# Last steps of the expert stage and the norm that opens the next layer

## The reference, cut to what matters

```python
def hier_moe(h, w_grp, w_exp, w1, w3, w2):      # 32 experts, 2 per token
    ...
    for e in range(N_EXPERTS):
        a = jax.nn.silu(ht @ w1[e]) * (ht @ w3[e])
        y = y + combine[:, e:e + 1] * (a @ w2[e]).astype(jnp.float32)
    ...
x = x + gt2[:, None, :] * hier_moe(h2, ...)     # first block's last line
...
def rmsnorm_2(x, g):
    y = xf * lax.rsqrt(jnp.mean(xf * xf, axis=-1, keepdims=True) + NORM_EPS)
    return (y * g).astype(x.dtype)
h = rmsnorm_2(x, norm_gains[0]);  z = h @ w_in  # splits: lru_x, lru_gate, q, k, v, swa_gate
```

## Time and profile before

| | us |
|---|---|
| median of 3 runs | 2454.22 (2449.99 to 2456.52) |
| profiled execution, its own time | 2448.66 |
| its span | 2446.8 |
| TensorE matmuls busy | 2104.9 (86%) |
| VectorE busy | 1214.5 (50%) |
| ScalarE busy | 898.2 (37%) |
| HBM read | 691.66 MB, 284 GB/s over the span |

### The profile page before, as it was taken

One profiled execution on the slowest core, in us unless ns is written; L12 is line 12 of the kernel. 1 busy time (PEld: TensorE's weight loads), 2 busy tenths in 40 slices (PEclk: granted clock), 3 DMA queues, 4 the chain that ended last, 5 costly groups with the idle time before them and its releaser, 6 DMA issues.

```text
span 2446.8 us, 38264 instructions
## 1 busy us (share of the span) xinstructions
PE 2104.9 (86%) x14524; PEld 1399.7 (57%) x14524; DVE 1214.5 (50%) x2205; ACT 898.2 (37%) x1382; POOL 0.2 (0%) x4
## 2 busy tenths in 40 slices
PE   5699998986887888887878887899989799998987
PEld 1377776862222222222222222799889799997887
DVE  1544785454333333333333334647875554477555
ACT  1333434441112111221112221546865444466543
POOL 0000000000000000000000000000000000000000
PEclk9899999998999999999999999899999899998999
DMA  9988775966999999999999997364445455543442
GB/s 378 404 310 300 255 279 194 340 245 273 422 422 421 422 422 422 422 422 422 422 422 422 422 422 299 113 199 146 137 140 179 129 172 182 181 139 107 134 128 97
DMA packets 135046, 695.44 MB, mean 284 GB/s; under 512 B 14992, under 2 KB 15120, under 8 KB 85264
## 3 DMA queue, kind: packets, MB, share of 16 engines
q1 hardware_dynamic: 134928, 693.81, 74.2%
HBM read 691.66 MB, written 2.10 MB: 284 GB/s over the span
## 4 chain that ended last, share of the span: by engine, by line
PE 50%; DMA 37%; DVE 7%; ACT 4%; issue 2%; SPq 1%; DVEq 0%; ACTq 0%
PE acc L1000 34%; DMA ring<-in_w 33%; DMA land<-in_stream_a 4%; PE acc L997 3%; PE psS L1226 3%; PE psO L1050 3%; DVE WL L1662 1%; ACT WH L1378 1%; SPq L880 1%; PE psM L1081 1%; ACT SB L1448 1%; DVE HL L1672 0%; PE psT L946 0%; PE psM L1214 0%; PE psM L1050 0%
## 5 line engine op out<-in xcount | busy, mean ns | idle before, releaser
L1000 PE MATMUL acc<-HH,WH 128*128 128x256 f32 x2552 | 749.0, 293 | 40.7 <-DVE HL L1684 15.4
L1000 PE MATMUL acc<-HH,WL 128*128 128x256 f32 x2552 | 727.9, 285 | 0.0
L1000 PE MATMUL acc<-HL,WH 128*128 128x256 f32 x2552 | 727.4, 285 | 0.0
L1662 DVE TENSOR_TENSOR WL<-land,WH 128x1024 fp32r<-128x1024 f32 (+1 forms) x350 | 425.6, 1216 | 420.6 <-ACT WH L1378 416.5
L1000 PEld LDWEIGHTS acc<-HH,WH 128*128 128x128 f32 x2552 | 495.3, 194 | 81.7 <-issue 14.5
L1000 PEld LDWEIGHTS acc<-HH,WL 128*128 128x128 f32 x2552 | 495.9, 194 | 3.3 <-issue 2.2
L1000 PEld LDWEIGHTS acc<-HL,WH 128*128 128x128 f32 x2552 | 495.4, 194 | 0.0
L1378 ACT ACTIVATE WH<-land 128x1024 fp32r<-128x1024 f32 (+1 forms) x350 | 368.0, 1051 | 248.6 <-PE acc L1000 198.9
L1226 PE MATMUL psS<-ring,low 128*32 128x512 f32 x2048 | 282.3, 664 | 148.9 <-DMA ring<-in_w 126.7
L1226 PEld LDWEIGHTS psS<-ring,low 128*32 128x32 f32 x2048 | 53.4, 113 | 339.3 <-DMA ring<-in_w 253.0
L2046 DVE TENSOR_REDUCE SB<-psT 128x128 f32<-128x512 f32 x32 | 22.1, 692 | 389.0 <-PE psT L1236 389.0
(11 more groups left out here) (326 smaller groups left out, 1989.0 us busy)
## 6 DMA issues: line engine op xcount, KB each, us to landing
ring<-in_w SPq DMA_DIRECT2D x384, 1024.0 KB, 24.1
land<-in_stream_a SPq DMA_DIRECT2D x284, 512.0 KB, 7.5
land<-in_stream_bc SPq DMA_DIRECT2D x246, 512.0 KB, 3.8
land<-in_stream_bc SPq DMA_DIRECT2D x12, 384.0 KB, 3.2
X<-in_xT SPq DMA_DIRECT2D x1, 2048.0 KB, 15.8
out<-low SPq DMA_DIRECT2D x4, 512.0 KB, 2.7
cst<-in_const SPq DMA_DIRECT2D x1, 1538.0 KB, 12.3
low<-in_w_pool SPq DMA_DIRECT2D x1, 1024.0 KB, 4.9
```

Source lines behind the costliest of these rows:

```text
L1000: mm = pe.matmul(bank[:, 0:S], w[:, kk, :], h[:, rows[kk], :], start=(z == 0 and i == 0), stop=stop)
L1662: ins = dve.tensor_tensor(WL[:, q % PARTS, 0:n], land[k][:, p % LAND[k], 0:n], WH[:, q % PARTS, 0:n].bitcast(F32), ALU.subtract)
```

## The change

What it does: (1) bankO is multiplied by a tile GB (the gate gt2 laid out in rows, made once by a VectorE copy, four matmuls and a ScalarE copy near the end of list A) when VectorE evacuates it to OE, and the scatter outputs are added into X itself; YT is gone. (2) The scatter of tile i-1 stands between the up-products: slot s, then output s. Outputs are numbered so that output m holds chunks `chunks_of(m)`. (3) VectorE takes the OE evacuation from ScalarE, and makes the first selection ahead of the clears. (4) The last tile's scatter belongs to BC: an addition "res", two HH copies and one 128x512 square for each output; X is not scaled by the norm's factor. The squares are added on VectorE (7 additions of 128x512), summed by two matmuls ("ssm") placed, with the two that turn the factor into a column ("rcol"), between the halves of the product bk1. (5) The factor is applied to bk, bs, lx, lg by a VectorE evacuation that multiplies by RT, to bv by ScalarE's scale, and to the queries in the softmax scale. bq stays a plain copy. (6) In BC the ring `land` moves to ring slots 0 to 3, WH and WL to slots 3 to 7, HH and HL to slots 7 to 11; the stream of layer two starts when the last tile's slots 0 to 3 are used, ScalarE's high parts after its slots 0 to 7. The first four low parts are computed by GpSimd. The count w_used starts at 12 (SLOTS), given by the clear of bankO, so each wait on it is written 12 higher.

```diff
+def evac_by(x):
+    return "dve" if x[0] in ("bk", "bs", "lx", "lg") else "act"
+def chunks_of(m):
+    return (8 * (m // 4) + m % 4, 8 * (m // 4) + m % 4 + 4)
 def order_bc():
-    o.load(1)
+    o.load(4, by="pool")
+    o.add("dve", "zero_b")
+    o.add("dve", "weigh_out")
+    for m in range(8):
+        o.add("pe", "scat", m)
+        for c in chunks_of(m):
+            o.add("act", "hh", "moe", c)
+        o.add("act", "sqm", m)
+    split = [c for m in range(8) for c in chunks_of(m)]
+    for m in range(8):
+        o.add("dve", "res", ("moe", m))
+        if m > 1:
+            o.add("dve", "hl", "moe", split.pop(0))
+    for c in split:
+        o.add("dve", "hl", "moe", c)
+    for m in range(1, 8):
+        o.add("dve", "sqsum", ("moe", m))
     o.misc.append(("ssum", "moe"))
-    for n in range(KD):
-        o.add("dve", "res", ("moe", n))
-        o.add("act", "sq", ("moe", n))
-        o.add("pe", "ss", ("moe", n))
-    o.load(1)
-    o.norm_input("moe")
-    o.load(2)
+    o.add("dve", "ssum", "moe")
+    o.add("act", "sqrtn", "moe")
+    o.add("dve", "rstd", "moe")
+    o.misc.append(("rcol",))
+    o.add("dve", "rcol")
     for n in range(2):
-        o.proj(("bk", n))
+        o.proj(("bk", n), after="sums" if n else None)
 # SyncE
-                    sp.wait_ge(moe["w_used"], i * SLOTS + (s + 1 - SLOTS))
+                    sp.wait_ge(moe["w_used"], i * SLOTS + (s + 1))
-            sp.wait_ge(moe["w_used"], tiles * SLOTS)
+            sp.wait_ge(moe["w_used"], tiles * SLOTS + 4)
             stream(1, BC, t["stream_bc"], tiles)
 # TensorE, the loop
                     mm.then_inc(moe["w_used"], 1)
+                    if s == 0:
+                        pe.wait_ge(moe["oe_ready"], i + 1)
+                        pe.wait_ge(moe["scj_ready"], i + 1)
+                    pe.wait_ge(moe["y_added"], i * 8 + s + 1)
+                    scatter(s).then_inc(moe["y_full"], 1)
...
-                scatter(i)
+                spread(i)
+                pe.wait_ge(moe["y_added"], i * 8 + 10)
+                gather_t(i + 1)
                 pe.wait_ge(moe["at_ready"], i + 2)
...
-                pe.wait_ge(moe["y_added"], i * 8 + 10)
-                gather_t(i + 1)
-                spread(i)
-            scatter(tiles)
             run(1, BC)
 # ScalarE
-                act.wait_ge(moe["w_used"], i * 12 + 12)
-                act.wait_ge(moe["y_full"], i * 8 + 8)
-                act.activation(OE, bankO, ACT.Copy).then_inc(moe["oe_ready"], 1)
-            act.wait_ge(moe["y_added"], tiles * 8 + 10)
+            act.wait_ge(moe["w_used"], tiles * SLOTS + 8)
             run(1, BC)
 # VectorE
-            dve.memset(OE, 0.0) ...; dve.memset(YT[:, 0:8, :], 0.0) ...; dve.memset(YT[:, 8:16, :], 0.0) ...
             pick(0, True)
+            dve.memset(bankO, 0.0) ...; (SJ in two halves, AT, H1T, H3T, SL1 as before)
             weigh(0, True)
             with dve.Fori(0, tiles) as i:
+                dve.wait_ge(moe["w_used"], i * SLOTS + SLOTS)
+                dve.tensor_tensor(OE, bankO, GB, ALU.mult).then_inc(moe["oe_ready"], 1)
                 pick(i + 1)
+                for m in range(8):
+                    add_out(m, i)
...
+                    elif what == "evac":
+                        bank = acc[o.acc.index(("proj", x)) % 2]
+                            ins = dve.tensor_tensor(W(at)[:, 0, :], bank[:, 0:S], RT, ALU.mult)
 # GpSimd
+                pool.tensor_tensor(WLs[1][:, q % PARTS, 0:n], land[1][:, p % LAND[1], 0:n],
+                                   WHs[1][:, q % PARTS, 0:n].bitcast(F32), ALU.subtract)
```

More of the change, by code:

```diff
@@ L204, in mix_head, with proj @@
         self.misc.append(("ssum", name))
-    def proj(self, x, halves=None, post=None, loads=1, between=None, first=0):
+    def proj(self, x, halves=None, post=None, loads=1, between=None, first=0, after=None):
         if halves is None:
@@ L220, in proj @@
                     between()
+                if after:
+                    self.add("pe", "ssm")
+                    self.add("pe", "rcol")
         self.acc.append(("proj", x))
-        self.add("act", "evac", x)
+        self.add(evac_by(x), "evac", x)
         if x[0] == "wi":
@@ L464, in order_a @@
         o.add("act", "h2", c)
+    o.add("dve", "gt2rows")
     o.add("pe", "router")
@@ L737, in program @@
         unit_in = [[sem(f"unit_in{k}_{i}") for i in range(LAND[k])] for k in range(2)]
-        done = [{e: sem(f"{e}_done{k}") for e in ("pe", "act", "dve")} for k in range(2)]
+        done = [{e: sem(f"{e}_done{k}") for e in ("pe", "act", "dve", "pool")} for k in range(2)]
         act_link, dve_link = sem("act_link"), sem("dve_link")
@@ L768, in program @@
         lam2 = small[:, 50:56]
+        rcol, rq = small[:, 202:204], small[:, 204:206]
         jst = small[:, 112:144].rearrange("p (b k h) -> p b k h", b=2, k=4)
@@ L981, in product @@
                     last = i == 1
-                needs(k, "dve", o, "lo", q)
+                needs(k, o.lo_by[q], o, "lo", q)
+                WH, WL, HH, HL = WHs[k], WLs[k], HHs[k], HLs[k]
                 wh, wl = (z[:, q % PARTS, cols].rearrange("p (k m) -> p k m", k=len(rows)) for z in (WH, WL))
-                terms = [(a, b, c, kk) for kk in range(len(rows)) for a, b, c in ((wh, HH, 0), (wl, HH, 1), (wh, HL, 2))]
+                order = range(len(rows))
+                if name == "bk":
+                    order = [c - rows[0] for m in range(4 * i, 4 * i + 4) for c in chunks_of(m)]
+                terms = [(a, b, c, kk) for kk in order for a, b, c in ((wh, HH, 0), (wl, HH, 1), (wh, HL, 2))]
                 normed = {("k", 0): "x", ("bk", 0): "moe", ("cq", 0): "wb"}.get(x)
@@ L2061, in _ @@
             dve.wait_ge(moe["y_added"], tiles * 8 + 2)
-            for m in range(8):
-                add_out(m, tiles)
-            dve.wait_ge(moe["y_added"], tiles * 8 + 10)
             dve.wait_ge(moe["j_ready"], tiles + 2)
             run(1, BC)
+        @block.gpsimd
+        def _(pool):
+            for count, (what, q) in enumerate(BC.steps["pool"]):
+                assert what == "lo"
+                if count:
+                    pool.wait_ge(done[1]["pool"], count)
+                p = BC.halves[q]
+                n = BC.pieces[p][2]
+                pool.wait_ge(done[1]["act"], BC.at["act"][("hi", q)])
+                pool.tensor_tensor(WLs[1][:, q % PARTS, 0:n], land[1][:, p % LAND[1], 0:n],
+                                   WHs[1][:, q % PARTS, 0:n].bitcast(F32), ALU.subtract).then_inc(done[1]["pool"], 1)
 def _unit(w):
```

236 lines of the change are left out of this document (150 added, 86 removed).

## The result

The changed kernel takes **2434.4 us** (median of 4 runs, 2431.95 to 2441.22), the kernel before 2454.97 beside it: ratio 0.9929, 95% interval 0.9913 to 0.9945. Taken again in another series it had 2437.5 and 0.9935 (0.9921 to 0.9949). The forecast was 2417: the direction was right, the gain about half of what was forecast, and the time lies just outside the range.

The account below looks back on a forecast made before the run. It took the expert loop as DMA-bound between two serial chains, and later layers as TensorE-bound. Terms -6.2 - 31.0 + 3.5 = -33.7 gave 2415 from the profile or 2420.5 from the median; forecast 2417, range 2404 to 2434.

Parts of the forecast that it names:

- What bounds the kernel, and the period of a tile: Expert loop: DMA-bound at 422 GB/s, 29.83 us a tile, with serial chains around it; layers behind bound by TensorE.
- rival 3: Expert loop: TensorE's chain at the lower clock outlasts the DMA, +55 us, 2470; chance 0.04.
- Part 1: Loop entry: selection ahead of the clears lets slot 0 be used earlier, -6.2 us (bounds -7.5 and -4).
- Part 2: Inside the expert loop: reordered matmuls stay hidden under the DMA, cost 0.
- steady chain of 23.3: Expert loop: TensorE's estimated time per tile in the new order at full clock, 6.5 us below 29.83.
- Part 3: Loop exit to bk1's second half: shorter chain gains 32.6 us, -31.0 after the clock (bounds -25 and -36).
- The 1.6 for the clock: Second half of bk1: 1.6 us taken from the exit's gain because it runs partly at the lower level.
- Part 4: Exit: GpSimd computes the first four low parts in time for TensorE, cost 0.
- rival 1: Exit: GpSimd and VectorE block each other, making VectorE about 3.3 us late, 2420; chance 0.18.
- Part 5: Stage of bs, lx, lg: 24 evacuations moved from ScalarE to VectorE cost +3.5 us (bounds 0 and +10).
- rival 2: Stage of bs, lx, lg: VectorE becomes the bound, evacuations and late banks show, +10 to +14, 2426; chance 0.13.
- three signs of being wrong: Tile period over 30 us, pause before bk1's second half over 10 us, bs/lx/lg stage growing by over 8 us.

Follow-up runs that it names:

- e3: Changed kernel with scatter products and additions back at their old place inside the loop; 2441.4 us, ratio 0.9954 to the kernel before.
- e0: Changed kernel timed again without any edit; 2437.5 us, ratio 0.9935 to the kernel before.
- e1: Changed kernel with bs, lx, lg evacuated raw by ScalarE and multiplied by the factor in SBUF by VectorE; 2427.4 us, ratio 0.9898 to the kernel before.
- e2: e1 without the 24 factor multiplications, so bs, lx, lg stay unscaled; 2425.9 us, ratio 0.9891 to the kernel before.
- e5: Changed kernel with GpSimd writing zeros instead of computing the first four low parts; 2438.4 us, ratio 0.9933 to the kernel before.
- e6: Changed kernel with squares summed by TensorE, column products behind bk1 and the root's table loaded early; 2433.4 us, ratio 0.9918 to the kernel before.
- e4: Changed kernel with five idle TensorE products ahead of the first gather; 2434.6 us, ratio 0.9921 to the kernel before.
- v4: v3b plus one idle 128x256 product in each pause ahead of slot 0; 2419.7 us, ratio 0.9868 to the kernel before.
- v2: Changed kernel with the edits of e1, e4 and e6, and two of four low parts moved back to VectorE; 2420.3 us, ratio 0.9862 to the kernel before.
- e8: Changed kernel with eight idle TensorE products ahead of the first gather; 2434.8 us, ratio 0.9917 to the kernel before.
- v3b: v2 with eight idle products instead of five, a repeat timing; 2419.2 us, ratio 0.9865 to the kernel before.

## Why the prediction was wrong, step by step

**What bounds the kernel, and the period of a tile**: right. 29.82 us at 422 GB/s; rival 3 is out.

**Part 1, -6.2**: measured -6.9. Right, though about 1.0 of it is not the change's: the router's five small products behind the mark ran at the full level in after (0.39 us each) and at the lower one in before (0.61). In e3, which has the same entry as after, they took 0.61 again, and slot 0 came 28.5 behind the mark.

**Part 2, "Cost 0"**: wrong by 6 us (5.4 over the other profiles). I compared the steady chain of 23.3 with 29.83. The first tiles are not steady: the queue is empty, and what counts is how soon the first slots are given back. With a scatter between slots at the lower level the first two came 3.9 us apart, against the 2.49 that the DMA needs for one, and all eight were used within 18.0 us, against 7.1 in before; the down-products began 23.7 us behind slot 0 instead of 17.9. The rate was 352 and 383 GB/s from 580 to 590 where before had 424 and 423. From slot 2 on the slots came every 2.06 us, faster than the DMA needs them, and the rate was low even so; what holds it down with few slots in the queue is not shown. Order and clock can be set side by side, slot 0 to landed: old order, full level 929.5 (before); old order, lower level 931.0 (e3); new order, lower level 934.6 to 935.5 (after, e0, e1, e2, e5, e6); new order, full level 930.8 and 932.5 (e4, v4). So the order costs some 4 at the lower level and 1 to 3 at the full one. The chain I had added up was short as well: a slot and its scatter take 2.06 at the full level, not 1.83. The new order is still worth having: it saves 6.7 at the exit (e3).

**Part 3, -32.6 before the clock**: measured -28.3. Of the 4.3 missing, 1.9 is a term that I had put at nothing: I set L = 1501.5 where the DMA rate falls and let TensorE use the last slot at once, but by the spacing of the slots TensorE can use it only at 1503.5. In before a scatter hid these 2 us, so counted from the landing as TensorE sees it the exit before was 60.0 long, not 62.0; in the new exit they stand on the chain. The other 2.4 are behind that, 31.8 instead of 29.4 (the terms I gave add up to 29.1): 1.8 is VectorE, late with HL and the sums (26.6 instead of 24.8), most of which e5 takes back. The 1.6 for the clock was about right (4.81 against 3.0).

**Part 4, "0"**: four low parts in 9.79 us, 2.45 each, were in time for TensorE. Their effect on VectorE was rival 1, given 3.3 us and measured at 1.4 to 1.8. The Trainium skill, "SBUF — State Buffer", section "Who interferes with whom", says that a VectorE instruction with two SBUF inputs and a GpSimd instruction that reads SBUF contend, and that one which only writes doesn't. The trace agrees: two HL took 1.74 us beside GpSimd's subtraction, and HL took 0.48 beside its writing of zeros and alone. The estimate of 2.3 us, worked out from the Trainium skill, "GPSIMD Engine Reference", section 3.1, stands beside 2.45 measured.

**Part 5, "+3.5 (bounds 0 and +10, all 24 exposed)"**: this is the step that failed. Measured 13.9 (e2), beyond its bound. I had written that "a bank is now free only when VectorE, in order, comes to it", and then priced it by the instructions' own time, 0.43 each, with the halves in WH/WL as a cushion. Those cushion TensorE against late weights, not against a late bank: with two banks, TensorE stops after one product. The price is what stands ahead of the exit in VectorE's queue: in e0 9.4 us of waits at three places, 7.8 in the first profile. To that come matmuls at the lower level, some 1.7 us more for each 48 behind the two long waits and 1.5 behind the second wait on HL. It is rival 2's size (+10 to +14). Rival 2 named two causes together, VectorE's load and the late banks; e1, which changes the second and leaves the first, took 10.2 back, e2 the other 3.7. Its headline, VectorE as the bound, was the smaller part; its "each late bank shows" was the larger. A reading in this part was off too: from 1720 to 1780 TensorE lost 2.0 us in before, not 3. Of the three signs of being wrong that I had named, only the last came: the period is 29.82, the pause before bk1's second half is 6.7 us, and the stage of bs, lx and lg grew by 11.7.

The sum: -6.2 forecast became -6.9 (0.7 better), 0 became +6.0, -32.6 became -28.3, +5.1 became +16.4: 21.0 us worse behind the router. The medians move by 15.4 to 20.6 and the profiles behind the router by 12.7. Only one profile of before exists, and its 2448.66 lies 6.3 below the median beside it; where in before the remaining 3 to 8 us lie stays open.

## What to carry to other kernels

Before an exit from PSUM is moved to another engine, list what stands ahead of it in that engine's order: the bank waits for all of it, and with two banks the matmul engine stops. A factor can be applied one step later, in SBUF, at almost the same cost in instructions, and no bank waits for it. And a stage bound by DMA still has a start: price the first tile with an empty queue and at the level that the profile shows there, not by the steady period.

## What was unexpected of the hardware

- Where the granted clock falls at the start of the loop is not settled by the length of single pauses: with 2.97, 0.72 and 0.86 us it stayed up (e4), with 3.09 it fell within the gather (v2), with 0.40, 0.72 and 1.02 it fell in slot 0 (e8 and v3b), and with the last two filled it held (v4).
- Behind waits of 3.5 to 3.7 us on TensorE 48 matmuls took 7.37 to 7.48 us in after instead of 5.76; behind one of 3.47 in before they took 5.97.
- Between the fall of the DMA rate and the moment at which TensorE can use the last slot lie about 2 us (1501.5 and 1503.5 in before, the second worked out from the spacing of the slots).
- The DMA rate stood at 352 and 383 GB/s while slots came back every 2.06 us, faster than the 2.49 at which they are filled at 422.
- The same first block of 540 us ended up to 8.3 us apart between executions, which is more than most of the edits studied here move.
